# Odd layer's recurrence: sigmoids computed as tanh, and two products whose 128 columns of weights are split into two column halves

## The chip, the cores and the metric

The kernel runs on one core of a Trainium2 chip. Everything is float32. The metric is the device time of one launch in microseconds (us); lower is better.

## The reference, cut to what matters

The program is three transformer blocks in a row on 512 tokens of width 1024. The change lies in the last layer only, the "odd" layer of the third block, in its RWKV-7 recurrence, which runs once forwards and once backwards over the tokens in 16 heads of 64 channels:

```python
def rwkv7_bidir_branch(p, mu, w0, w2, a0, a2, k_k, k_a, r_k, lnx_g, lnx_b):
    q = pf[None] + mu[:, None, None, :] * (shifted - pf[None])
    r, k, v, wd, ad = jnp.split(q, RWKV_SPLITS, axis=-1)
    z_w = w0[:, None, None, :] + jnp.einsum('dbsl,dlc->dbsc', jnp.tanh(wd), w2)
    decay = jnp.exp(-jnp.exp(-jax.nn.softplus(-z_w) - 0.5))      # = exp(-exp(-0.5) * sigmoid(z_w))
    a = jax.nn.sigmoid(a0[:, None, None, :] + jnp.einsum('dbsl,dlc->dbsc', ad, a2))
    kk = heads(k * k_k)
    kk = kk * lax.rsqrt(jnp.maximum(jnp.sum(kk * kk, axis=-1, keepdims=True), 1e-12))
    k = k * (1.0 + (a - 1.0) * k_a)
    ...
def wkv7_step(state, inp):          # scanned over the 512 tokens, with a = -kk, b = kk * a
    r, w, k, v, a, b = inp
    sa = jnp.einsum('...ij,...j->...i', state, a)
    state = (state * w[..., None, :] + sa[..., :, None] * b[..., None, :]
             + v[..., :, None] * k[..., None, :])
    y = jnp.einsum('...ij,...j->...i', state, r)
```

## The kernel before, in words

Each engine has its own instruction list, written out by hand in Python; semaphores between them are numbered by a dry run. The order on an engine is the order in which its generators yield, and no scheduler changes it. ScalarE (ACT) gets a table load wherever the next function isn't in the table set that is loaded.

The recurrence is computed in chunks of 128 tokens, 4 chunks (`NT`) in a sequence. Work is cut into 16 items `i`: item `i` is feature tile `ft = i // 2` (128 channels, so two heads of 64) in direction `d = i % 2`. An item has three stages, and `rw_rounds` runs in one round the chain of item `r`, the inverse of item `r+1` and the products of item `r+2`, interleaved piece by piece, on each of TensorE (PE), ScalarE and VectorE (DVE):

- products (`pe_rw_products`, `act_rw_products`, `dve_rw_products`). PE makes the low-rank products of the decay and of `a` (line 2896). ACT takes their sigmoids into `t_sg` and `t_al` (2961, 2964). DVE scans `t_sg` over a chunk into a running sum `Pc` (3032), takes its tail (3035) and the sum less its middle (3041); ACT makes from them the exponentials s1, s2, s3 (2972, 2973, 2975) and `t_ep`, `t_en` (2978, 2979). Line 2864 and 2869 mix a stream with its shifted self, 2986 squares k, 2846 sums over a head, 2989 takes a root (its own table set), 2857 spreads the result over 64 rows. DVE then forms the four features FM: L3058, L3063 (`b = kk * a`), L3064, L3066, L3069, L3071 (`b` times a decay), L3073, L3078, L3079. PE transposes (2914), multiplies features (2928), and DVE masks the products (`copy_predicated`, 3099). At the end come "rhs own" (line 2946, the masked matrix times the item's own values, 64 columns for each head) and "y own" (2949).
- inverse (`pe_inverse` and its ACT and DVE parts, lines 818 to 939): the triangular inverse of each 128x128 block by doubling, with 64x64 products (833, 849, 861, 869, 878), transposes (818) and copies by ACT (887, 892, 896, 901, 906).
- chain (`pe_rw_chain` and its parts): four steps `n` that depend on each other through the state. A step makes rhs (3168, DVE 3239), u (line 3179: the inverse times rhs, for each of two heads; copied by ACT 3216 in step 0 and by DVE 3244 later), the state update (3187, 3189, DVE 3254 or 3256, 3261) and y (3195, 3197). After every second item DVE, ACT and PE normalise the result (3269 to 3287).

A float32 matmul of the program stands in the trace as two PE records with two weight loads (PEld). So the 8 matmuls of "rhs own" are x16, and the 2 of a u step are x4. "128\*64" in a trace row is the part of the array in use, rows by columns: 128 rows and 64 columns of weights.

POOL zeroes the targets of the masks (3127) and starts inverses (914). After round 13, the last two rounds have no products; other layers' matmuls (line 272) stand beside the chain there.

Of the kernel before, what the change touches and what calls it, by code (L numbers as in the profile page):

```python
# [18 lines left out]
C0 = math.exp(-0.5)  # L19
# [171 lines left out]
def assemble(nc, ctx, io, out):  # L191
# [22 lines left out]
    cols = 53215 - 21 * 128 - NPAR - NROW - 4 * 2048 - 8 * 516 - 64 - 64  # L214
# [10 lines left out]
    def mem_of(ap, width):  # L225
        return View(ap.rearrange("p (a b) -> p a b", b=width))
# [9 lines left out]
    def par(name, k=0):  # L236
        return params[:, PCOL[name] + k:PCOL[name] + k + 1]
# [10 lines left out]
    def bank(*step):  # L248
        return PS[banks.of.get(step, 0)]
# [2559 lines left out]
    om = lambda i: OM[:, i:i + 1]  # L2809
    wv = [mem_of(w, TOK) for w in wbuf]  # L2810
# [74 lines left out]
    def pe_rw_products(pe, i):  # L2885
# [49 lines left out]
        for name, kind in (("rw rhs own", 1), ("rw y own", 2)):  # L2935
            b, before = banks.take(name, i)
            if before:
                pe.wait_ge(*at("out", *before))
            for hd in range(2):
                pe.wait_ge(*at("out", "rw ms", i, 4 * hd + kind))  # L2940
            for c in range(NT):
                s_ = slice(c * 128, (c + 1) * 128)
                for hd in range(2):
                    vs = VK(0)[:, c * 128 + 64 * hd:c * 128 + 64 * hd + 64]
                    if kind == 1:
                        t = pe.mm(PS[b][:, c * 128 + 64 * hd:c * 128 + 64 * hd + 64], MS[hd](1)[:, s_], vs,  # L2946
                                  start=True, stop=True)
                    else:
                        t = pe.mm(PS[b][H2[hd], s_], vs, MS[hd](2)[:, s_], start=True, stop=True)
            t.then_inc(pe.inc(s, "mm", name, i), 1)  # L2950
            yield

    def act_rw_products(a, i):
# [4 lines left out]
        if i:  # L2958
            a.wait_ge(*at("rw kr", i - 1))
        a.wait_ge(*at("mm", "rw w", i))  # L2960
        a.act(t_sg, bank("rw w", i), ACT.Sigmoid, bias=par("o_w0_3", 8 * d + ft)).then_inc(
            a.inc(s, "out", "rw w", i), 1)
        a.wait_ge(*at("mm", "rw a", i))
        a.act(t_al, bank("rw a", i), ACT.Sigmoid, bias=par("o_a0_3", 8 * d + ft)).then_inc(
# [7 lines left out]
        a.act(u3(s1), mdl if d == 0 else u3(s3), ACT.Exp, scale=-C0).then_inc(a.inc(s, "rw s1", i), 1)  # L2972
        a.act(u3(s2), u3(s3) if d == 0 else mdl, ACT.Exp, scale=-C0).then_inc(a.inc(s, "rw s2", i), 1)
        a.wait_ge(*at("rw s2", i))
        a.act(u3(s3), tot, ACT.Exp, scale=-C0).then_inc(a.inc(s, "rw s3", i), 1)
        yield
        a.wait_ge(*at("rw pc", i))
        a.act(t_ep, t_pc, ACT.Exp, scale=-C0).then_inc(a.inc(s, "rw ep", i), 1)
        a.act(t_en, t_pc, ACT.Exp, scale=C0).then_inc(a.inc(s, "rw en", i), 1)
# [39 lines left out]
    def dve_rw_products(v, i):  # L3019
# [11 lines left out]
        for c in range(NT):  # L3031
            v.scan(Pc[:, c, 1:129], ones, t_sg[:, c * 128:(c + 1) * 128], 0.0, MUL, ADD).then_inc(v.inc(s, "rw scan", i), 1)
# [30 lines left out]
        v.tt(FM(3), FM(0), t_al, MUL).then_inc(v.inc(s, "rw b", i), 1)  # L3063
        v.ts(t_al, t_al, par("o_k_a_3", ft), om(50 + ft), MUL, ADD).then_inc(v.inc(s, "rw al", i), 1)  # L3064
# [6 lines left out]
        v.tt(c3(FM(3)), c3(FM(3)), e_k, MUL).then_inc(v.inc(s, "rw f4", i), 1)  # L3071
# [82 lines left out]
    def pe_rw_chain(pe, i):  # L3154
# [5 lines left out]
        for n, c in enumerate(ssd_order(d)):  # L3160
# [17 lines left out]
            for hd in range(2):  # L3178
                t = pe.mm(PS[b][:, 64 * hd:64 * hd + 64], DT(hd)[:, s_], rhs[:, 64 * hd:64 * hd + 64],  # L3179
                          start=True, stop=True)  # L3180
# [159 lines left out]
    def dve_rwkv(v):  # L3340
# [4 lines left out]
        v.ts(OM[:, 50:58], params[:, PCOL["o_k_a_3"]:PCOL["o_k_a_3"] + 8], -1.0, 1.0, MUL, ADD).then_inc(  # L3345
            v.inc(s, "rw mix"), 1)
        v.fill(Pc[:, :, 0:1], 0.0).then_inc(v.inc(s, "rw pc pad"), 1)
# [194 lines left out]
```

## Time and profile before

| | |
|---|---|
| time, median of 3 runs | 4971.45 us (4971.11 to 4972.32) |
| profiled execution, its own time | 4975.08 us |
| its span, first to last instruction | 4973.3 us |
| recurrence, first product to last "rhs own" group | about 3929 to 4690 us of the span |
| PE busy over the span | 4589.2 us (92%) |
| ACT, DVE busy over the span | 845.3 us (17%), 2548.8 us (51%) |
| granted PE clock over the span | 0.928 |

The span of 4973.3 us lies 1.8 us under its execution's own time, and that time lies 3.6 us above the median of the three timed runs. The granted clock is a share of 2.4 GHz: 1.00 is 2.4 GHz, 0.50 is 1.2 GHz, and a value between is a mixture of the two. A row of the chain of waits is start, duration and what ran; a row of the timeline is start, duration, engine, line, operation, operands and count, and behind it the engine's idle time before it with what ended that.

### The profile page before, as it was taken

Reading aid. Unit: us, or ns where it says so; the run is one execution under the profiler, and the core shown is the slowest. Engines: PE = TensorE matmul, PEld = TensorE weight load, DVE = VectorE, ACT = ScalarE, POOL = GpSimd, SP = SyncE. Lnnn points to the kernel's source line nnn. Section 1 sums busy time; section 2 is a strip of 40 time slices with the busy share of each in tenths; the row PEclk is TensorE's granted clock in tenths of the full one; section 3 lists DMA queues with packets and bytes.
Section 4 is the critical chain, followed back from the end, with each engine's and each line's share of the span. In section 5 each row is a group of like instructions: output and inputs, shape, how many; then the busy total and the mean of one; then the engine's idle time right before and its main releaser. Section 6 shows DMA issues by size and latency. Waiting matters only on the chain.

```text
span 4973.3 us, 64889 instructions
## 1 busy us (share of the span) xinstructions
PE 4589.2 (92%) x28316; PEld 3408.7 (69%) x28316; DVE 2548.8 (51%) x4403; ACT 845.3 (17%) x1490; POOL 123.6 (2%) x228
## 2 busy tenths in 40 slices
PE   9999998879998999799989999989999788888899
PEld 7886445557886888356656488858887666666644
DVE  5675865334545456553344265556454355555511
ACT  0001023111022000321222100011000233333210
POOL 0000000000000000000000000000000011111000
PEclk9998999868999999899999999989899888878899
DMA  6524442004222222111111222222222000000021
GB/s 238 179 94 58 65 65 51 1 1 85 93 86 67 85 91 87 36 41 51 51 43 35 68 85 85 68 85 86 67 88 77 27 2 2 2 2 2 19 96 42
DMA packets 284954, 311.69 MB, mean 63 GB/s; under 512 B 7168, under 2 KB 277632, under 8 KB 281600
## 3 DMA queue, kind: packets, MB, share of 16 engines
q1 hardware_dynamic: 284672, 307.55, 21.7%
q8 instruction: 223, 3.65, 0.3%
q14 instruction: 59, 0.48, 0.0%
HBM read 305.43 MB, written 2.10 MB: 62 GB/s over the span
## 4 chain that ended last, share of the span: by engine, by line
PE 49%; DVE 5%; ACT 3%; issue 1%; DMA 0%; POOL 0%; DVEq 0%; POOLq 0%; ACTq 0%; SPq 0%
PE ps L348 18%; PE ps L272 13%; PE ps L2125 1%; PE ps L317 1%; PE ps L833 1%; PE ps L471 1%; PE ps L2928 1%; PE ps L2857 1%; PE ps L849 1%; PE ps L3179 1%; PE ps L2846 1%; PE ps L2946 1%; PE ps L818 1%; PE ps L1845 1%; PE ps L2665 1%
## 5 line engine op out<-in xcount | busy, mean ns | idle before, releaser
L272 PE MATMUL ps<-main,w 128*128 128x512 f32 (+1 forms) x2832 | 1245.2, 596 | 21.9 <-DMA w<-in_ffn_wg 12.2
L348 PE MATMUL ps<-main 128*128 128x256 f32 x5136 | 1139.2, 379 | 0.0
L348 PEld LDWEIGHTS ps<-main 128*128 128x128 f32 x5136 | 975.5, 190 | 133.1
L272 PEld LDWEIGHTS ps<-main,w 128*128 128x128 f32 x2832 | 543.2, 195 | 647.3 <-issue 619.6
L348 PE MATMUL ps<-main,w 128*128 128x256 f32 x3872 | 863.9, 379 | 1.4 <-DVE main L416 1.4
L348 PEld LDWEIGHTS ps<-main,w 128*128 128x128 f32 x3872 | 736.1, 190 | 105.8 <-issue 4.3
L435 DVE TENSOR_TENSOR main<-main,ps 128x512 f32<-128x512 f32 x164 | 112.8, 688 | 417.7 <-PE ps L348 417.5
L661 DVE SCALAR_TENSOR_TENSOR main<-main,params_sb 128x512 f32<-128x512 f32 x256 | 192.5, 752 | 9.1
L387 ACT COPY main<-ps 128x256 f32<-128x256 f32 x98 | 36.5, 372 | 896.3 <-PE ps L348 896.3
L432 DVE TENSOR_TENSOR main<-main,ps 128x512 f32<-128x512 f32 x98 | 67.3, 687 | 221.6 <-PE ps L348 218.8
L440 DVE TENSOR_TENSOR main<-main,ps 128x512 f32<-128x512 f32 x164 | 112.8, 688 | 78.0 <-PE ps L348 76.7
L397 DVE TENSOR_TENSOR main<-w 128x512 f32<-128x512 f32 (+1 forms) x164 | 111.2, 678 | 31.2 <-DMA w<-in_w_in 11.8
L849 PE MATMUL ps<-main 64*64 64x64 f32 x3200 | 86.7, 261 | 32.2 <-ACT main L892 26.4
L402 DVE TENSOR_TENSOR main<-w,main 128x512 f32<-128x512 f32 (+1 forms) x164 | 112.4, 686 | 5.6
L400 DVE TENSOR_TENSOR main<-main,w 128x512 f32<-128x512 f32 (+1 forms) x164 | 112.4, 685 | 5.7
L398 DVE TENSOR_TENSOR main<-w 128x512 f32<-128x512 f32 (+1 forms) x164 | 111.1, 677 | 0.0
L849 PEld LDWEIGHTS ps<-main 64*64 64x64 f32 x3200 | 71.9, 167 | 54.7 <-issue 24.3
L387 ACT COPY tmp<-ps 128x256 f32<-128x256 f32 x66 | 24.6, 372 | 498.9 <-PE ps L348 498.9
L533 ACT ACTIVATE tmp<-main 128x512 f32<-128x512 f32 x104 | 63.8, 629 | 266.1 <-DVE main L585 79.0
L2179 DVE TENSOR_TENSOR main<-main 128x512 f32<-128x512 f32 x56 | 38.8, 692 | 135.3 <-PE ps L2125 126.9
L3099 DVE COPY_PREDICATED w<-consts_sb,ps 128x512 f32<-128x512 uint32 x128 | 85.6, 724 | 43.3 <-PE ps L2928 43.3
L818 PE MATMUL ps<-consts_sb,main 128*128 128x128 f32 x400 | 83.1, 343 | 23.0 <-DVE main L919 23.0
(456 smaller groups left out, 4985.2 us busy)
## 6 DMA issues: line engine op xcount, KB each, us to landing
w<-in_w_in SPq DMA_DIRECT2D x58, 1024.0 KB, 7.0
w<-in_e_w_in SPq DMA_DIRECT2D x28, 1024.0 KB, 5.0
main<-in_ada_w SPq DMA_DIRECT2D x24, 1024.0 KB, 5.0
w<-in_ffn_wg SPq DMA_DIRECT2D x22, 1024.0 KB, 6.4
w<-in_ffn_wu SPq DMA_DIRECT2D x22, 1024.0 KB, 6.3
w<-in_o_w_in SPq DMA_DIRECT2D x20, 1024.0 KB, 5.5
w<-in_ffn_wd SPq DMA_DIRECT2D x16, 1024.0 KB, 5.1
w<-in_w_up SPq DMA_DIRECT2D x16, 1024.0 KB, 5.5
```

The costliest lines, as they stand in the source:

```text
L272: i = pe.mm(PS[b][:, 0:n], wv[:, k, f * 128:(f + 1) * 128], g.X(kg + k), start=kg + k == 0, stop=kg + k == g.nk - 1)
L348: t = pe.mm(PS[b][:, 256 * half:256 * half + 256], weight[:, m, :], x(m), start=m == 0, stop=m == n - 1)
L397: v.tt(S[0], a21, a22, ADD).then_inc(v.inc(s, "sum 0", *step), 1)
L398: v.tt(S[2], a21, a11, SUB).then_inc(v.inc(s, "sum 2", *step), 1)
L400: v.tt(S[1], S[2], a22, ADD).then_inc(v.inc(s, "sum 1", *step), 1)
L402: v.tt(S[3], a12, S[1], SUB).then_inc(v.inc(s, "sums", *step), 1)
L435: v.tt(inner, two(c[3]), b[2], ADD).then_inc(v.inc(s, "most", *step), 1)
L440: v.tt(inner, inner, b[3], ADD).then_inc(v.inc(s, "out", "seven", 3, *step), 1)
L661: v.stt(out, src[:, j:j + TOK], w(j), out, MUL, ADD).then_inc(v.inc(s, "tap", j, *step), 1)
L818: t = pe.tp(part128(PS[b], n), part128(src, n), ident)
L849: t = pe.mm(PS[two[e][0]][HALF[q], 64 * n:64 * n + 64], E4[HALF[e], n, q, :], X4[HALF[e], n, q, :], start=True, stop=True)
L3099: v.pick(c3(MS[hd](kind)), mid(const(strict if kind < 2 else incl), 4).bitcast(U32), c3(bank("rw ms", i, k))).then_inc(v.inc(s, "out", "rw ...
```

## The change

Sigmoid(x) is (1 + tanh(x/2)) / 2. ACT now computes tanh of half the argument, with halved biases that DVE prepares once in a small tile `HW` (two more DVE instructions at the start). The factor 1/2 and the added 1 are taken up by what follows: the scan adds `ones` at each step instead of multiplying by it (`ADD, ADD`), so the running sum is twice the old one, and the five exponentials have half the scale; `b` is `(tanh + 1) * kk`, halved where it is multiplied by its decay; the constants of the line that makes `1 + (a - 1) k_a` are halved. Two `tensor_tensor` become `scalar_tensor_tensor`.

In "rhs own" (kind 1) and in the u step, each matmul with 128 columns of weights becomes two with 64 columns of weights each, for the upper and the lower half of the output's partitions, one straight after the other. All 128 rows and all 64 moving columns stay.

`cols` now counts the constants by `NCON`, so that `main` has room for `HW`; nothing else moves in memory.

```diff
@@ -2943,8 +2945,9 @@  (pe_rw_products)
                     if kind == 1:
-                        t = pe.mm(PS[b][:, c * 128 + 64 * hd:c * 128 + 64 * hd + 64], MS[hd](1)[:, s_], vs,
-                                  start=True, stop=True)
+                        for h in HALF:
+                            t = pe.mm(PS[b][h, c * 128 + 64 * hd:c * 128 + 64 * hd + 64],
+                                      part128(MS[hd](1), c)[:, h], vs, start=True, stop=True)
@@ -2957,11 +2960,12 @@  (act_rw_products)
+        a.wait_ge(*at("rw half"))
         a.wait_ge(*at("mm", "rw w", i))
-        a.act(t_sg, bank("rw w", i), ACT.Sigmoid, bias=par("o_w0_3", 8 * d + ft)).then_inc(
+        a.act(t_sg, bank("rw w", i), ACT.Tanh, scale=0.5, bias=hw(8 * d + ft)).then_inc(
...
-        a.act(t_al, bank("rw a", i), ACT.Sigmoid, bias=par("o_a0_3", 8 * d + ft)).then_inc(
+        a.act(t_al, bank("rw a", i), ACT.Tanh, scale=0.5, bias=hw(16 + 8 * d + ft)).then_inc(
...
-        a.act(u3(s1), mdl if d == 0 else u3(s3), ACT.Exp, scale=-C0).then_inc(a.inc(s, "rw s1", i), 1)
+        a.act(u3(s1), mdl if d == 0 else u3(s3), ACT.Exp, scale=-C0 / 2).then_inc(a.inc(s, "rw s1", i), 1)
...
@@ -3029,7 +3033,7 @@  (dve_rw_products)
-            v.scan(Pc[:, c, 1:129], ones, t_sg[:, c * 128:(c + 1) * 128], 0.0, MUL, ADD).then_inc(v.inc(s, "rw scan", i), 1)
+            v.scan(Pc[:, c, 1:129], ones, t_sg[:, c * 128:(c + 1) * 128], 0.0, ADD, ADD).then_inc(v.inc(s, "rw scan", i), 1)
...
-        v.tt(FM(3), FM(0), t_al, MUL).then_inc(v.inc(s, "rw b", i), 1)
-        v.ts(t_al, t_al, par("o_k_a_3", ft), om(50 + ft), MUL, ADD).then_inc(v.inc(s, "rw al", i), 1)
+        v.stt(FM(3), t_al, 1.0, FM(0), ADD, MUL).then_inc(v.inc(s, "rw b", i), 1)
+        v.ts(t_al, t_al, hw(32 + ft), om(50 + ft), MUL, ADD).then_inc(v.inc(s, "rw al", i), 1)
...
-        v.tt(c3(FM(3)), c3(FM(3)), e_k, MUL).then_inc(v.inc(s, "rw f4", i), 1)
+        v.stt(c3(FM(3)), c3(FM(3)), 0.5, e_k, MUL, MUL).then_inc(v.inc(s, "rw f4", i), 1)
@@ -3176,8 +3180,9 @@  (pe_rw_chain)
             for hd in range(2):
-                t = pe.mm(PS[b][:, 64 * hd:64 * hd + 64], DT(hd)[:, s_], rhs[:, 64 * hd:64 * hd + 64],
-                          start=True, stop=True)
+                for h in HALF:
+                    t = pe.mm(PS[b][h, 64 * hd:64 * hd + 64], part128(DT(hd), c)[:, h], rhs[:, 64 * hd:64 * hd + 64],
+                              start=True, stop=True)
@@ -3342,8 +3347,12 @@  (dve_rwkv)
+        v.ts(HW[:, 0:32], params[:, PCOL["o_w0_3"]:PCOL["o_w0_3"] + 32], 0.5, None, MUL).then_inc(
+            v.inc(s, "rw half w"), 1)
+        v.ts(HW[:, 32:40], params[:, PCOL["o_k_a_3"]:PCOL["o_k_a_3"] + 8], 0.5, None, MUL).then_inc(
+            v.inc(s, "rw half"), 1)
```

Two places show what it does to the instruction lists. The first is ACT at the start of item 3's products, from the first function after the low-rank products to the copy for the inverse. Before:

```order
L2961 ACT_TABLE_LOAD [waits pe_rwkv]
L2961 ACTIVATE tmp<-ps,params_sb 128x512 [waits dve_rwkv]
L2964 ACTIVATE tmp<-ps,params_sb 128x512 [waits pe_rwkv]
L3216 ACTIVATE main<-ps 128x128 [waits pe_rwkv]
L2972 ACT_TABLE_LOAD
L2972 ACTIVATE small<-small 128x4 [waits dve_rwkv]
L2973 ACTIVATE small<-main 128x4
L2975 ACTIVATE small<-main 128x4 [waits act_rwkv]
L887 COPY main<-ps 128x512 [waits pe_rwkv]
```

The same place in the changed kernel (line 2965 is the old 2961, 2968 the old 2964, 3221 the old 3216, 2976 to 2979 the old 2972 to 2975):

```order
L2965 ACT_TABLE_LOAD [waits pe_rwkv]
L2965 ACTIVATE tmp<-ps,main 128x512 [waits dve_rwkv]
L2968 ACTIVATE tmp<-ps,main 128x512 [waits pe_rwkv]
L3221 ACTIVATE main<-ps 128x128 [waits pe_rwkv]
L2976 ACTIVATE small<-small 128x4 [waits dve_rwkv]
L2977 ACTIVATE small<-main 128x4
L2979 ACTIVATE small<-main 128x4 [waits act_rwkv]
L887 COPY main<-ps 128x512 [waits pe_rwkv]
```

The load ahead of the exponentials is gone, the one ahead of the tanh stays where the one ahead of the sigmoid was. Over the whole program the table loads go from 94 to 77: one in each of the 16 items, and in the first item both, since a tanh stands ahead of it already.

The second place is PE in the round that follows, from the end of one item's products into the chain's first u step and, further on, its second. Before:

```order
L2946 MATMUL ps<-main,w 128x64 x7
L2949 MATMUL ps<-w,main 64x128 x8
L2896 MATMUL ps<-main 128x512 x2
L3179 MATMUL ps<-main 128x64 [waits act_rwkv,dve_rwkv]
L3179 MATMUL ps<-main 128x64
...
L2846 MATMUL ps<-consts_sb,tmp 128x2 x3
L3179 MATMUL ps<-main 128x64 [waits dve_rwkv]
L3179 MATMUL ps<-main 128x64
L833 MATMUL ps<-main,w 64x64 [waits dve_rwkv]
```

In the changed kernel (2949, 2952, 2898, 3184 and 2848 are the old 2946, 2949, 2896, 3179 and 2846):

```order
L2949 MATMUL ps<-main,w 64x64 x15
L2952 MATMUL ps<-w,main 64x128 x8
L2898 MATMUL ps<-main 128x512 x2
L3184 MATMUL ps<-main 64x64 [waits act_rwkv,dve_rwkv]
L3184 MATMUL ps<-main 64x64 x3
...
L2848 MATMUL ps<-consts_sb,tmp 128x2 x3
L3184 MATMUL ps<-main 64x64 [waits dve_rwkv]
L3184 MATMUL ps<-main 64x64 x3
L833 MATMUL ps<-main,w 64x64 [waits dve_rwkv]
```

In these rows 128x64 is the output, partitions by columns, and a matmul counts once. The places, the waits and the neighbours are the same; 8 matmuls became 16 and 2 became 4.

## Rows read from the trace of the kernel before

**Rows 1.** Busy by stretch: start:end, length, busy of PE, PEld, DVE, ACT, POOL, PEclk.
```profile
3929.50:4690.00 760.50, 626.38 (x9235) 504.24 (x9236) 432.77 (x1072) 275.77 (x476) 108.89 (x183) 0.82 0.01 2
4230.00:4246.00 16.00, 14.57 (x292) 12.49 (x291) 10.22 (x24) 4.48 (x8) 2.70 (x3) 1.00 0.01 2
4252.00:4275.00 23.00, 18.51 (x253) 15.17 (x254) 14.88 (x41) 10.19 (x19) 1.42 (x3) 0.61 0.01 2
```

**Rows 2.** Chain of waits over 3929.5 to 4690 us, its shares by line.
```profile
by line: PE ps L2928 5.5%; PE ps L2857 5.2%; PE ps L833 5.2%; PE ps L471 5.2%; PE ps L849 4.7%; PE ps L3179 4.5%; PE ps L2846 4.4%; PE ps L2946 4.2%; PE ps L818 3.5%; PE ps L2896 3.0%; DVE tmp L2869 2.8%; ACT L2972 2.7%; DVE main L914 2.4%;
```

**Rows 3.** The same chain in order of time, parts of one round.
```profile
4253.66 1.28 ACT L2972
...
4261.10 0.95 PE ps L3179 x4
...
4272.64 1.09 PE ps L3179 x4
...
4274.79 2.00 PE ps L471 x2
...
4294.60 1.93 PE ps L2946 x16
4296.53 0.84 PE ps L2846 x8
```

**Rows 4.** Timeline of ACT, DVE and PE around the load of line 2972.
```profile
4252.93 1.37 DVE L3032 TENSOR_TENSOR_SCAN main<-consts_sb,tmp 128x128 f32<-128x128 f32 x4 [6.42 <-ACT tmp L2961]
4253.66 1.28 ACT L2972 ACT_TABLE_LOAD   x1
4254.33 0.17 DVE L3035 TENSOR_TENSOR small<-main 128x4 f32<-128x4 f32 x1
4254.61 0.70 DVE L3041 TENSOR_TENSOR tmp<-main,small 128x516 f32<-128x516 f32 x1
4254.95 0.21 ACT L2972 ACTIVATE small<-small 128x4 f32<-128x4 f32 x1
4255.87 0.64 ACT L2978 ACTIVATE tmp<-tmp 128x516 f32<-128x516 f32 x1
4256.02 1.13 PE L833 MATMUL ps<-main,w 64*64 64x64 f32 x32 [0.91 <-ACT main L887]
```

**Rows 5.** Timeline of PE, 128\*64 work of another stage with 64 moving columns.
```profile
2408.05 3.89 PE L2125 MATMUL ps<-main 128*64 128x64 f32 x64 [3.77 <-ACT main L2102]
...
2477.20 1.15 PE L2150 MATMUL ps<-main 128*64 128x64 f32 x16
...
2486.21 2.16 PE L2125 MATMUL ps<-main 128*64 128x64 f32 x64
```

**Rows 6.** Timeline of PE where 128\*128 work is followed by 128\*64 work.
```profile
4738.69 0.39 PE L3189 MATMUL ps<-main 128*128 128x128 f32 x2
4738.91 0.39 PE L3195 MATMUL ps<-main 128*128 128x128 f32 x2
4739.23 0.44 PE L3197 MATMUL ps<-w,main 128*64 128x128 f32 x4
```

**Rows 7.** Timeline of PE and DVE around u steps and what follows them.
```profile
4226.86 0.74 DVE L3079 SCALAR_TENSOR_TENSOR tmp<-tmp,params_sb 128x512 f32<-128x512 f32 x1
4227.81 2.07 PE L471 MATMUL ps<-tmp,consts_sb 128*128 128x512 f32 x2
...
4260.96 1.09 PE L3179 MATMUL ps<-main 128*128 128x64 f32 x4
4261.98 1.13 PE L833 MATMUL ps<-main,w 64*64 64x64 f32 x32
...
4273.47 0.74 DVE L3079 SCALAR_TENSOR_TENSOR tmp<-tmp,params_sb 128x512 f32<-128x512 f32 x1
```

**Rows 8.** Groups of instructions on DVE, the two forms that are exchanged.
```profile
L3063 DVE TENSOR_TENSOR w<-main,tmp 128x512 f32<-128x512 f32 x16 | 11.1, 692 | 0.5
...
L758 DVE SCALAR_TENSOR_TENSOR main<-main 128x512 f32<-128x512 f32 x16 | 10.3, 688 | 0.3
```

More of the change, by code:

```diff
@@ L213, in assemble @@
     small = sb("small", [128, 64])
-    cols = 53215 - 21 * 128 - NPAR - NROW - 4 * 2048 - 8 * 516 - 64 - 64
+    cols = 53215 - NCON - NPAR - NROW - 4 * 2048 - 8 * 516 - 64 - 64
     main = sb("main", [128, cols])[:, :]
@@ L2809, in assemble @@
     om = lambda i: OM[:, i:i + 1]
+    HW = mem(37184, 1, 64).ap[:, 0, :]
+    hw = lambda i: HW[:, i:i + 1]
     wv = [mem_of(w, TOK) for w in wbuf]
@@ L2971, in act_rw_products @@
         a.wait_ge(*at("rw tail", i))
-        a.act(u3(s1), mdl if d == 0 else u3(s3), ACT.Exp, scale=-C0).then_inc(a.inc(s, "rw s1", i), 1)
-        a.act(u3(s2), u3(s3) if d == 0 else mdl, ACT.Exp, scale=-C0).then_inc(a.inc(s, "rw s2", i), 1)
+        a.act(u3(s1), mdl if d == 0 else u3(s3), ACT.Exp, scale=-C0 / 2).then_inc(a.inc(s, "rw s1", i), 1)
+        a.act(u3(s2), u3(s3) if d == 0 else mdl, ACT.Exp, scale=-C0 / 2).then_inc(a.inc(s, "rw s2", i), 1)
         a.wait_ge(*at("rw s2", i))
-        a.act(u3(s3), tot, ACT.Exp, scale=-C0).then_inc(a.inc(s, "rw s3", i), 1)
+        a.act(u3(s3), tot, ACT.Exp, scale=-C0 / 2).then_inc(a.inc(s, "rw s3", i), 1)
         yield
         a.wait_ge(*at("rw pc", i))
-        a.act(t_ep, t_pc, ACT.Exp, scale=-C0).then_inc(a.inc(s, "rw ep", i), 1)
-        a.act(t_en, t_pc, ACT.Exp, scale=C0).then_inc(a.inc(s, "rw en", i), 1)
+        a.act(t_ep, t_pc, ACT.Exp, scale=-C0 / 2).then_inc(a.inc(s, "rw ep", i), 1)
+        a.act(t_en, t_pc, ACT.Exp, scale=C0 / 2).then_inc(a.inc(s, "rw en", i), 1)
         yield
@@ L3344, in dve_rwkv @@
         v.ts(OM[:, 0:50], mu, -1.0, 1.0, MUL, ADD).then_inc(v.inc(s, "rw mix mu"), 1)
-        v.ts(OM[:, 50:58], params[:, PCOL["o_k_a_3"]:PCOL["o_k_a_3"] + 8], -1.0, 1.0, MUL, ADD).then_inc(
+        v.ts(OM[:, 50:58], params[:, PCOL["o_k_a_3"]:PCOL["o_k_a_3"] + 8], -0.5, 1.0, MUL, ADD).then_inc(
             v.inc(s, "rw mix"), 1)
+        v.ts(HW[:, 0:32], params[:, PCOL["o_w0_3"]:PCOL["o_w0_3"] + 32], 0.5, None, MUL).then_inc(
+            v.inc(s, "rw half w"), 1)
+        v.ts(HW[:, 32:40], params[:, PCOL["o_k_a_3"]:PCOL["o_k_a_3"] + 8], 0.5, None, MUL).then_inc(
+            v.inc(s, "rw half"), 1)
         v.fill(Pc[:, :, 0:1], 0.0).then_inc(v.inc(s, "rw pc pad"), 1)
```

## The prediction, made before the changed kernel ran

> **What bounds the kernel now.** I read the busy times by stretch first, then the chain of waits, then the timeline where the chain passes the changed lines. The whole program is bound by PE (92% of the span), but the change lies in one stretch of 760 us, and there PE is busy for 626 us only, at a granted clock of 0.82 [rows 1]. So time is lost in two ways there: PE waits for ACT and DVE, and after such waits it runs for a while at 1.2 instead of 2.4 GHz (a clock of 0.61 between 4252 and 4275 us, where ACT and DVE hand work to and fro, against 1.00 between 4230 and 4246 us, where PE is busy for 14.6 of 16 us [rows 1]). The chain of waits in this stretch is a mixture of short pieces of all three engines, of which the changed lines hold: u (L3179) 4.5%, "rhs own" (L2946) 4.2%, the table load (L2972) 2.7% [rows 2]. In order of time the reader is to see that each round (760 us for 16 items) passes through one load, one L2946 and three u steps, of which the load, two u steps and L2946 are shown [rows 3].
>
> **Part 1, the table load.** There are 16 loads of 1.28 us ahead of the exponentials, all on the chain (2.7% of 760 us is 20.5 us) [rows 2, 3]. Not all of it is won. The exponential behind the load needs DVE's tail, L3035, which ends at 4254.50, while the load ends at 4254.94 [rows 4]: the scan (4 instructions, 1.37 us) runs beside the load. Without it the exponential starts at about 4254.53, 0.42 us earlier than 4254.95. The next possible stop is L2978, which needs L3041 (ends 4255.31) and would then stand at 4255.87 - 0.42 = 4255.45, so it isn't held [rows 4]. Two things are released by this ACT stretch: PE's L833 through the copy L887, for which it waits 0.91 us [rows 4], and the mixing of k, so the 0.42 us is on the path. The other 14 rounds show the same distances within 0.02 us; only in item 0 DVE's L3041 ends with the load, and nothing is won. Sum: 15 x 0.42 = 6.3 us. Bounds: 0 (if PE's own queue were the limit, which its wait speaks against) and 16 x 1.28 = 20.5 us. The load ahead of the tanh stays, and its waits too. The load that goes in item 0 stood beside the low-rank products and hid there.
>
> The Trainium skill (ScalarE: Activation LUTs, "What ACT_TABLE_LOAD costs") counts a switch at about 2.66 us, of which 1.38 us is a drain. The trace doesn't agree: the activation behind the load starts 1.29 us after the load [rows 4]. By that rule the sum would not change either where DVE's tail is the next to be waited for.
>
> **Part 2, the form of the products.** No row shows these two lines in the new form, but L2125 is that form exactly: 128 rows, 64 columns of weights, 64 moving columns, the two column halves in turn. It takes 2.16 us for 64 records, 0.034 us each, at full clock, and 3.89 us, 0.061 us each, after a wait at the low one [rows 5]. L2946 takes 1.93 us for 16 records, 0.12 us each, and L3179 0.95 to 1.09 us for 4 at the low clock [rows 3]. The count of records doubles.
>
> A change between forms of the array costs something. L3189 and L3195 are both 128\*128 and start 0.22 us apart; L3195 and the 128\*64 L3197 start 0.32 us apart, for as many records [rows 6]. So 0.10 us for a change at full clock.
>
> "Rhs own": 32 x 0.034 = 1.08 us instead of 1.93, 0.85 us less. In items of direction 0 the next work (L2949) is 128\*64 too, and a change goes away rather than comes. In the others L2846 (128\*128) stands behind it [rows 3], one change more, 0.75 us less. All 16 are on the chain (4.2% of 760 us is 31.9 us, 2.0 us each [rows 2]). Nothing that follows is late: the masks and transposes that L2949 and L2846 need are done before L2946 starts. Sum: 8 x 0.85 + 8 x 0.75 = 12.8 us.
>
> u, step by step. Step 0 is followed by a wait for ACT (L3216 behind the two sigmoids), step 3 by DVE's masks and by L3244 queued behind them: nothing is won. Step 1 runs after L2846 and ahead of L833; start to start it takes 1.02 us [rows 7]. New: 8 x 0.061 = 0.49 us, and two changes instead of one, at the low clock perhaps 0.15 us each, an estimate from the 0.10: about 0.8 us, 0.2 us less. At full clock (3 rounds of 14) 8 x 0.034 us plus 0.2 leaves 0.1 us. Step 2 is the same, but L471 behind it needs DVE's L3079: in most rounds that ends at 4274.21 against a start of L471 at 4274.79 on the chain [rows 3, 7], so there is room for 0.2 us; in the three rounds like the one at 4227 us it ends at 4227.60 against 4227.81, and less a hand-over of 0.14 us only 0.07 us is left [rows 7]. Sum: step 1 gives 11 x 0.2 + 3 x 0.1 = 2.5 us, step 2 gives 11 x 0.2 + 3 x 0.07 = 2.4 us, together 4.9 us. Bounds: 22 x 0.53 = 11.7 us if changes of form cost nothing (1.02 - 0.49), and 0 if they cost all. In the last two rounds u stands between the full-array products of line 272; eight narrow records and two changes cost what four wide ones do. Nothing.
>
> **Part 3, DVE.** Two tensor_tensor become scalar_tensor_tensor with a constant: 692 against 688 ns [rows 8], so 0. A scan that adds instead of multiplies, other constants and a bias from another tile: 0. Two small instructions at the start stand beside the load of the low-rank weights, for which PE waits: 0. If each of the two exchanged forms cost the 0.05 us more that forms with a per-channel scalar show (0.74 us [rows 7]), it would be 1.6 us.
>
> **Sum.** 6.3 + 12.8 + 4.9 = 24.0 us. The profiled execution took 4975.1 us in all, span 4973.3; it would be 4951.1. It lies 3.6 us above the median of the timed runs, 4971.45, so I predict 4947 us.
>
> **Rivals.**
> Halves don't overlap. L2150 has the same form, but all the records of a group go to one half: 1.15 us for 16, 0.072 us each [rows 5]. If the new lines ran at that pace, "rhs own" would take 2.3 us, 0.37 us more, 16 times 5.9 us; u about 0.2 us more, 28 times 5 us; with part 1 taken off, about 5 us slower: 4976 us. Against it stands L2125, whose order of halves is the one that is written here. The Trainium skill (TensorE: Matmul & The Clock Gate, "Part 3: Packing small matmuls") says that weight loads overlap running matmuls only when the row group differs, and both halves have the same rows; by that rule this rival would hold. L2125's 0.034 us beside L2150's 0.072 us says that it doesn't. Chance 6%.
>
> Changes of form cost more than I count. Then u gives nothing and "rhs own" some 9 us: 6.3 + 9 = 15 us, 4956 us. For it: pieces of one form between others are everywhere in a round, and 0.10 us comes from one place. Chance 22%. The Trainium skill (TensorEngine Tiling, "Key Properties") says that changing the tiling mode drains the TensorE; rows 6 agree in sign with 0.10 us.
>
> They cost less, and u gives its bound: 6.3 + 13 + 11 = 30 us, 4941 us. Chance 16%.
>
> The slower side: the clock. PE gets less to do before each wait. If a quarter of the 14.6 us that PE works at full clock between 4230 and 4246 us [rows 1] fell to 1.2 GHz in every round, that would add 15 x 3.6 = 55 us: 31 us slower, 5002 us. It decides from 24/15 = 1.6 us of such work a round, and is slower by more than 0.2% from 2.3 us on. For it: the clock does fall in every round, to 0.61 in the stretch that follows [rows 1], and nothing in the trace says how near to falling it is before that. Against it: the wait gets shorter by part 1, and the work is as dense as before. Chance 5%. A smaller drift of the clock that gives back 14 to 24 us: 6%, about 4966 us.
>
> The table load would not go: the instruction list shows that it does.
>
> **Numbers.** The forecast has 45%, with a range of its own of 4940 to 4954. Faster by over 0.2% (10 us, about what can be told from no change) are it and the two variants: 83%. Within 0.2%: halves that don't overlap and the smaller drift, 12%. Slower: 5%. The range of 8 in 10 runs from 4936 to 4962.
>
> **What would show it.** L2946's line x512 in 128\*64 form, about 1.1 us a group, busy some 18 us instead of 33; L3179's x512, at the low clock about 0.7 to 0.8 us start to start; no load on line 2976, and the exponential 0.03 us behind DVE's tail; rounds of about 47 us; PEclk of the stretch within 0.02 of 0.82. I am wrong if the narrow records take 0.07 us each, if the clock of the stretch falls below 0.79, or if the chain goes through other engines at the place of L2946.

## The result, and the profile after

The changed kernel takes 4927.01 us (median of 4 runs, 4925.46 to 4934.56), the kernel before beside it 4971.89 us (4971.11 to 4972.49): a ratio of 0.9913, 95% interval 0.9896 to 0.993, or 44.9 us less. The forecast was 4947 us with a range of 4936 to 4962. The direction was right, the size nearly double, and the time lies below the range.

| | before | after |
|---|---|---|
| profiled execution, its own time | 4975.08 us | 4927.05 us |
| span | 4973.3 us | 4925.3 us |
| from the first low-rank product to the end | 1043.8 us | 999.7 us |
| of it at 1.2 GHz ("low"), summed from the trace's clock record | 286.7 us in 37 pieces | 238.9 us in 33 pieces |
| mean round of the recurrence (14 rounds) | 48.1 us | 45.3 us |

A piece of low time that reaches into this stretch is counted whole; the last piece, in which the program ends, is left out.

44.1 of the 48.0 us between the two profiled executions lie in the recurrence and what follows; 3.9 us lie ahead of it, in code that is the same.

The changed lines answer to [rows 3, 5, 8] as groups by form (busy us and mean ns behind the bar, then idle time before them):

```profile
L3184 PE MATMUL ps<-main 128*64 128x64 f32 x512 | 34.8, 269 | 4.2 <-DVE main L3244 4.0
L2949 PE MATMUL ps<-main,w 128*64 128x64 f32 x512 | 18.4, 224 | 1.5 <-DVE w L3103 1.5
L3067 DVE SCALAR_TENSOR_TENSOR w<-tmp,main 128x512 f32<-128x512 f32 x16 | 11.1, 692 | 0.5
L3075 DVE SCALAR_TENSOR_TENSOR w<-w,tmp 128x512 f32<-128x512 f32 x16 | 10.9, 684 | 0.0
L471 PE MATMUL ps<-tmp,consts_sb 128*128 128x512 f32 x44 | 34.9, 885 | 24.8 <-DVE tmp L491 16.8 <-DVE tmp L3083 7.9
```

The same groups before:

```profile
L3179 PE MATMUL ps<-main 128*128 128x64 f32 x256 | 53.2, 344 | 8.7 <-DVE main L3239 8.6
L2946 PE MATMUL ps<-main,w 128*128 128x64 f32 x256 | 32.9, 283 | 1.5 <-DVE w L3099 1.5
L471 PE MATMUL ps<-tmp,consts_sb 128*128 128x512 f32 x44 | 41.4, 1041 | 24.0 <-DVE tmp L491 16.8 <-DVE tmp L3079 7.1
```

"Rhs own" (L2949) is busy for 18.4 us, where L2946 had 32.9; u (L3184) for 34.8 us, where L3179 had 53.2. The exchanged DVE forms cost what the old ones did. But L471, which nobody changed, went from 41.4 to 34.9 us.

The start of a round answers to [rows 4]:

```profile
4228.95 1.37 DVE L3036 TENSOR_TENSOR_SCAN main<-consts_sb,tmp 128x128 f32<-128x128 f32 x4 [5.14 <-ACT tmp L2965]
4230.35 0.17 DVE L3039 TENSOR_TENSOR small<-main 128x4 f32<-128x4 f32 x1
4230.55 0.20 ACT L2976 ACTIVATE small<-small 128x4 f32<-128x4 f32 x1 [0.89 <-DVE small L3039]
4231.47 0.64 ACT L2982 ACTIVATE tmp<-tmp 128x516 f32<-128x516 f32 x1
```

The load is gone, ACT now waits 0.89 us for DVE's tail L3039, and the exponential starts 0.03 us behind it. From the scan to L2982 it is 2.52 us, before it was 2.94: 0.42 us, as forecast.

The u step and "rhs own", answering to [rows 3, 7]; the second fence is from the chain of waits:

```profile
4236.63 0.70 PE L3184 MATMUL ps<-main 128*64 128x64 f32 x8
4237.26 1.13 PE L833 MATMUL ps<-main,w 64*64 64x64 f32 x32
...
4258.98 0.45 PE L3184 MATMUL ps<-main 128*64 128x64 f32 x8
4259.36 0.69 PE L833 MATMUL ps<-main,w 64*64 64x64 f32 x32
```

```profile
4269.63 1.08 PE ps L2949 x32
4270.71 0.98 PE ps L2848 x8
```

u takes 0.63 us start to start at the low clock (1.02 before, 0.8 forecast) and 0.38 at the full one; "rhs own" 1.08 us, where the chain before had 1.93 [rows 3].

Where else did time go? Item 4's round in both kernels, cut in pieces of 15 us (the columns are those of [rows 1]; the number behind POOL's is the granted clock). Before, then after:

```profile
4154.89:4169.89 15.00, 11.75 (x151) 9.80 (x155) 7.28 (x23) 8.79 (x16) 1.49 (x4) 0.66 0.00 1
4169.89:4184.89 15.00, 11.03 (x164) 8.38 (x164) 11.04 (x28) 2.77 (x5) 0.00 (x0) 0.77 0.00 1
4184.89:4199.89 15.00, 14.84 (x262) 12.53 (x263) 9.21 (x19) 3.55 (x6) 3.23 (x4) 1.00 0.01 3
4199.89:4207.19 7.30, 5.86 (x45) 3.80 (x44) 2.46 (x5) 2.57 (x5) 3.85 (x8) 0.68 0.01 2
```

```profile
4139.74:4154.74 15.00, 11.60 (x154) 9.41 (x154) 7.83 (x24) 7.51 (x15) 1.50 (x4) 0.66 0.01 1
4154.74:4169.74 15.00, 12.30 (x252) 9.85 (x254) 11.37 (x31) 3.36 (x6) 0.00 (x0) 0.89 0.01 2
4169.74:4184.74 15.00, 13.30 (x246) 11.08 (x240) 9.07 (x20) 5.17 (x9) 5.16 (x9) 1.00 0.01 2
```

The clock falls in the same place at the start of the round. Later it is back earlier (0.89 against 0.77), and the fall that ended the old round (0.68) doesn't come. Lines that are the same in both kernels show what that is worth. Before, then after:

```profile
4177.27 2.07 PE L471 MATMUL ps<-tmp,consts_sb 128*128 128x512 f32 x2
...
4203.17 1.97 PE L2857 MATMUL ps<-consts_sb,main 128*64 128x128 f32 x16 [1.44 <-DVE main L3280]
4205.07 2.08 PE L2896 MATMUL ps<-main 64*128 64x512 f32 x4
```

```profile
4161.15 1.13 PE L471 MATMUL ps<-tmp,consts_sb 128*128 128x512 f32 x2
...
4184.18 1.09 PE L2859 MATMUL ps<-consts_sb,main 128*64 128x128 f32 x16 [1.43 <-DVE main L3285]
4185.20 1.13 PE L2898 MATMUL ps<-main 64*128 64x512 f32 x4
```

Each of the three is 0.9 us shorter because TensorE runs at 2.4 instead of 1.2 GHz. No term of the forecast held such a gain.

### The profile page after: what moved, and what is told of

Read it like the earlier page. It is cut to its first block, busy times and chain, and to the rows that moved or that the text cites. A ratio compares the mean times of both kernels' runs of the same rounds, so it can differ in the third digit from the quotient of the medians.

```text
span 4925.3 us, 65898 instructions
## 1 busy us (share of the span) xinstructions
PE 4542.3 (92%) x28828; PEld 3368.0 (68%) x28828; DVE 2548.0 (52%) x4405; ACT 823.5 (17%) x1473; POOL 123.7 (3%) x228
## 4 chain that ended last, share of the span: by engine, by line
PE 48%; DVE 5%; ACT 3%; issue 1%; DMA 0%; POOL 0%; DVEq 0%; POOLq 0%; ACTq 0%; SPq 0%
PE ps L348 19%; PE ps L272 13%; PE ps L2125 1%; PE ps L317 1%; PE ps L833 1%; PE ps L2930 1%; PE ps L2859 1%; PE ps L2848 1%; PE ps L471 1%; PE ps L849 1%; PE ps L818 1%; PE ps L1845 1%; PE ps L2665 1%; PE ps L1834 1%; DVE main L3036 0%
## 5 line engine op out<-in xcount | busy, mean ns | idle before, releaser
L348 PEld LDWEIGHTS ps<-main,w 128*128 128x128 f32 x3872 | 736.1, 190 | 105.8 <-issue 4.3
L397 DVE TENSOR_TENSOR main<-w 128x512 f32<-128x512 f32 (+1 forms) x164 | 111.2, 678 | 31.2 <-DMA w<-in_w_in 12.3
```

Of the source, the lines that this page charges most:

```text
L348: t = pe.mm(PS[b][:, 256 * half:256 * half + 256], weight[:, m, :], x(m), start=m == 0, stop=m == n - 1)
L397: v.tt(S[0], a21, a22, ADD).then_inc(v.inc(s, "sum 0", *step), 1)
```

## The experiments

Theory: the change is worth in place about what was forecast (24 us), and the rest of the 45 us is time at 1.2 GHz that no longer occurs. Rival: all of it is work saved in place, and a term was mis-sized. "In place" means: at the changed lines themselves, with the clock the same in both kernels. "Low" is the time at 1.2 GHz of the profiled execution, counted as in the table above; before has 286.7 us of it.

| kernel | us, median (lowest to highest) | ratio to before, 95% | low, us |
|---|---|---|---|
| tanh only | 4971.23 (4968.22 to 4974.45) | 0.9998 [0.9989, 1.0007] | 303.8 |
| rhs own in halves only | 4958.42 (4956.39 to 4959.32) | 0.9974 [0.9963, 0.9984] | 276.5 |
| u in halves only | 4959.50 (4955.84 to 4961.09) | 0.9974 [0.9965, 0.9984] | 266.2 |
| both halves | 4939.87 (4938.36 to 4942.24) | 0.9937 [0.9922, 0.9952] | 249.2 |
| all three (the change) | 4927.01 (4925.46 to 4934.56) | 0.9913 [0.9896, 0.993] | 238.9 |
| halves in a row | 4936.59 (4929.94 to 4937.59) | 0.9929 [0.9913, 0.9946] | 228.7 |
| head sums in halves | 4902.52 (4901.61 to 4903.38) | 0.9864 [0.9849, 0.9879] | 208.2 |
| one matmul more | 4932.75 (4931.48 to 4934.33) | 0.9925 [0.991, 0.994] | 221.9 |
| two matmuls more | 4958.25 (4954.01 to 4960.55) | 0.9975 [0.9964, 0.9985] | 276.5 |
| before, filled | 4926.25 (4924.88 to 4927.78) | 0.9912 [0.9897, 0.9927] | 95.6 |
| tanh only, filled | 4919.83 (4913.78 to 4919.92) | 0.9896 [0.9881, 0.991] | 105.8 |
| after, filled | 4893.82 (4886.38 to 4895.16) | 0.9843 [0.9829, 0.9858] | 75.1 |
| filled at the products' waits | 4924.56 (4919.28 to 4924.78) | 0.99 [0.9886, 0.9915] | 204.8 |
| filled at the chain's waits | 4900.23 (4893.78 to 4910.26) | 0.9856 [0.984, 0.9872] | 88.7 |
| before, filled, head sums in halves | 4909.36 (4908.05 to 4911.81) | 0.9871 [0.9855, 0.9888] | 88.7 |
| after, filled, head sums in halves | 4869.02 (4862.97 to 4870.38) | 0.9794 [0.9779, 0.9809] | 47.8 |

### The parts of the change, each alone

The two products put back to their old form in the changed kernel (tanh only); here the edit in "rhs own", the one in u is its like:

```diff
-                        for h in HALF:
-                            t = pe.mm(PS[b][h, ...], part128(MS[hd](1), c)[:, h], vs, start=True, stop=True)
+                        t = pe.mm(PS[b][:, ...], MS[hd](1)[:, s_], vs, start=True, stop=True)
```

> The changed kernel with the wide form of both products put back: only the tanh part is left. Theory A (each edit saves in its own place what the trace of the changed kernel shows there, and what is left of the 45 us comes from TensorE's clock, which falls and rises at other places once the rounds have another length): 0.41 us a round in place, 6 us, so 4966 us, give or take some 10 us of clock that need not have the sign of the edit; the load on the line of the exponentials gone, the exponential 0.41 us earlier, and whatever differs beyond that sits in PE pieces that run at 1.2 in one kernel and 2.4 GHz in the other. Theory B (the parts simply are worth more than I priced, and add up to 45 us): 10 to 15 us faster, spread evenly over the rounds, and the time at the low clock as before.

Its first 700 us of the recurrence:

```profile
3924.60:4624.60 700.00, 579.03 (x8450) 465.04 (x8450) 399.55 (x991) 234.16 (x423) 100.70 (x171) 0.81 0.01 2
```

From the first function of a round to the exponential it takes 2.32 us instead of 2.74, in all rounds but the first two (2.58 before), and yet the kernel isn't faster: the clock is 0.81, with 17 us more at 1.2 GHz. This was the first sign that the clock matters as much as the work.

The other way round, one product at a time in the kernel before, and both:

```diff
-                        t = pe.mm(PS[b][:, ...], MS[hd](1)[:, s_], vs, start=True, stop=True)
+                        for h in HALF:
+                            t = pe.mm(PS[b][h, ...], part128(MS[hd](1), c)[:, h], vs, start=True, stop=True)
```

> The kernel before with the column halves in rhs own alone. Theory A: 16 groups of 1.1 instead of 2.0 us, 13 us in place, 4959 us, plus or minus the clock's share. Theory B: 18 to 22 us faster. Either way the line's busy time falls from 32.9 to about 18 us.

> The kernel before with the column halves in the u step alone. Theory A: 0.17 us in step 1 and up to 0.28 us in step 2 of each of 14 rounds, 4 to 6 us, 4966 us, plus or minus the clock's share. Theory B: the line is busy 18 us less in the changed kernel, so 15 to 18 us faster, 4955 us.

> The kernel before with the column halves in both products, and the sigmoids kept. Theory A: 13 + 6 = 19 us in place, 4953 us, and the sum of the differences of e1, e2 and e3 misses the 45 us of the whole change by several us, since the clock's share doesn't add up. Theory B: about 4972 - 45 + (what e1 gives), and e2 and e3 add up to it within 3 us.

Measured: 13.5, 12.5 and 32.1 us less than before. For u alone and for both, neither theory had the number (4 to 6 or 15 to 18 us expected for u). The three parts alone add up to 0.7 + 13.5 + 12.5 = 26.7 us; the whole gives 44.9. So the parts aren't additive, and what is missing in the sum is missing in the low time too. Alone, the parts change it by +17.1, -10.2 and -20.5 us, 13.6 us less together; the whole takes 47.8 us off. At 0.4 us for each microsecond at the low clock, a price that is worked out below, these 34.2 us are 14 of the 18.2 us that are missing.

### TensorE's waits filled

The waits of TensorE were filled with useless matmuls. They (256 columns, a constant times the identity, into an unused half of the bank, where nobody reads it) stand ahead of five waits in each item. The comments in this cut are added here.

```diff
+    def pe_fill(pe, b, n, o=256):
+        for _ in range(n):
+            pe.mm(PS[b][:, o:o + 256], ident, consts[:, 0:256], start=True, stop=True)
...
+        if name[0] == "rw kk":            # head sums of k
+            pe_fill(pe, b, 1)
...
+        if name[0] == "rw rstd all":      # spread behind the root
+            pe_fill(pe, b, 3)
...
+                if n == 2:                # third rhs of the chain
+                    pe_fill(pe, b, 3)
...
+                if n == 0:                # first state update
+                    pe_fill(pe, b, 3)
...
+            if m == 2 and name[0] == "rw":    # the inverse's second level
+                pe_fill(pe, two[0][0], 2)
```

> The kernel before with full-array matmuls of no use put into the places where PE waits in a round (3 ahead of the first state update, 2 ahead of the inverse's first product, 1 ahead of the head sums of k, 3 ahead of the third rhs, 3 ahead of the spread in the normalising; each writes columns of a bank that nobody reads). Theory A (the clock's share): PE's granted clock in the recurrence rises from 0.82 to 0.90 or more, the first L471 of a round takes 1.1 instead of 2.0 us, and the kernel gets 20 to 50 us faster although it does more. Theory C (what was gained beyond the priced terms has nothing to do with the clock): the clock may rise, the time doesn't fall below 4968 us.

> The changed kernel with the same matmuls in the same places. Theory A: with the clock held up in both, the difference between this and the filled kernel before is what the edits save in place, about 20 to 25 us (0.41 us of ACT, 0.85 us of rhs own and about 0.3 us of u a round), and no longer 45 us. Theory C: the difference stays 40 us or more.

> The kernel before with the tanh instead of the sigmoids and with the useless matmuls at TensorE's waits, products in their old form. Its partner is the kernel before with these matmuls, 4926.25 us. Theory (the tanh saves 0.41 us in place in 15 items, and without the filling the clock took this back): 6 us less than the partner, 4916 to 4923 us. Rival (the saving of 0.41 us is not on the path, it only lengthens a wait elsewhere): 4926 us, no difference to the partner within 2 us.

The same 700 us, of before filled and of after filled:

```profile
3927.00:4627.00 700.00, 616.72 (x9448) 490.75 (x9450) 426.58 (x1065) 273.01 (x471) 108.69 (x183) 0.94 0.01 2
```

```profile
3927.40:4627.40 700.00, 614.54 (x10444) 483.63 (x10444) 444.04 (x1113) 257.02 (x465) 108.74 (x183) 0.95 0.01 4
```

The kernel before gets 45.2 us faster by work that nobody needs, while the clock rises from 0.82 to 0.94. That the clock is worth tens of microseconds here is shown by this. The tanh, worth 0.7 us without the filling, is worth 6.4 us with it (4926.25 less 4919.83). That this is the forecast's 6.3 is partly luck: the low time differs by 10.2 us, the other way. At 0.4 us for each, the profiled executions of the two tanh pairs, from the first low-rank product to the end, give 7.0 us in place with the filling (2.9 + 4.1) and 7.4 without (0.6 + 6.8). The whole change is worth 32.4 us, above the 20 to 25 expected: the low time still differs by 20.5 us. All five places cost something too: the low time falls by 191 us, at 0.4 some 76, and the time only by 45.

### A pair nearly without time at the low clock

Filling and the head sums of line 2846 in column halves, on both kernels:

```diff
-            t = pe.mm(PS[b][:, 2 * c:2 * c + 2], x[:, c * 128:(c + 1) * 128], head_sums, start=True, stop=True)
+            for h in HALF:
+                t = pe.mm(PS[b][h, 2 * c:2 * c + 2], part128(x, c)[:, h], head_sums, start=True, stop=True)
```

> The changed kernel with the useless matmuls at TensorE's waits and with the head sums in two column halves. It tells whether the 24.5 us that the head sums in halves gave were in place or the clock's. In place they measured 26.7 less 16.0, that is 10.7 us, at a mixed clock; with the clock held up (0.95) the same records are shorter, so 6 to 11 us: 4883 to 4888 us. Rival (all 24.5 us are in place, behind the sums): 4869 us. It is also the fastest version that the runs so far point to.

> The kernel before with the useless matmuls at TensorE's waits and the head sums in two column halves: the partner of the changed kernel with both, 4869.02 us, whose recurrence spends 41 us at the low clock. Between these two the clock should have little part, so the difference is what the change is worth in place. Theory (the change gives 24 to 27 us in place: tanh 6, rhs own 12.6, u 5 to 9; the rest of the measured 45 us was the clock): 4893 to 4897 us, if the time at the low clock comes to 40 to 60 us here too. Rival (all of the 45 us are in place): 4914 us.

In medians the pair stands 40.3 us apart, not 24 to 27: the kernel before with both took 4909.36 us, not 4893 to 4897, nearer to what the rival said (4914). But its low time isn't the 40 to 60 us that the theory asked for, it is 88.7, and the two still differ by 40.9 us. The rounds tell work and clock apart. Of the kernel before with both:

```profile
4183.73:4225.86 42.13, 38.35 (x636) 31.11 (x637) 26.39 (x68) 17.52 (x31) 6.23 (x11) 1.00 0.01 2
4225.86:4271.60 45.74, 40.97 (x655) 32.09 (x653) 29.12 (x74) 17.66 (x31) 7.89 (x15) 0.96 0.01 2
4362.90:4404.74 41.84, 38.06 (x635) 30.85 (x636) 26.38 (x68) 17.52 (x30) 5.94 (x11) 1.00 0.01 2
4404.74:4451.59 46.85, 42.73 (x656) 33.18 (x654) 29.21 (x74) 17.67 (x31) 8.19 (x16) 0.93 0.01 2
4493.79:4538.01 44.22, 39.73 (x656) 31.03 (x654) 29.03 (x74) 17.67 (x32) 8.19 (x16) 1.00 0.01 2
```

Of the changed kernel with both:

```profile
4449.54:4492.03 42.49, 37.95 (x685) 29.34 (x685) 29.02 (x74) 16.38 (x30) 8.19 (x16) 1.00 0.01 3
4492.03:4532.31 40.28, 36.31 (x671) 29.04 (x672) 26.33 (x68) 16.23 (x30) 5.95 (x11) 1.00 0.01 2
```

Rounds at full clock from end to end are 41.84 and 44.22 us (the two directions) before, 40.28 and 42.49 after: 1.56 and 1.73 us less, 1.65 on average, 24.7 us for 15 rounds. The forecast's sum was 24.0. The 24.7 us are good to about 2 us: the row of 42.13 us is at 1.00 too, and with such rounds in the mean the sum is up to 1.2 us larger; and with the head sums in halves "rhs own" saves 0.95 us in both directions, in the change itself 0.75 us in one of them (below), about 1.4 us less in all. The same rows price the clock. Of three rounds of one direction the one at 1.00 takes 44.22 us, the one at 0.96 takes 45.74, the one at 0.93 takes 46.85. By the clock 0.04 of 45.74 us is 2 × 0.04 × 45.74 = 3.7 us at 1.2 GHz for 1.52 us of time, and 2 × 0.07 × 46.85 = 6.6 us for 2.63 us: 0.4 us for each microsecond at the low clock. With it the pair adds up: from the first low-rank product to the end the profiled executions are 40.5 us apart (983.2 and 942.7), and 24.7 + 0.4 × 40.9 = 41.1.

The Trainium skill (TensorE: Matmul & The Clock Gate, "HAM oscillation — how this bites in real kernels") counts half of the throttled time as lost. The rounds agree in kind and give 0.4. TensorE is busy for 40.97 of the 45.74 us of such a round, so part of the low time can fall on its waits; that this makes the difference isn't shown.

The expectation of the changed one was wrong: 4883 to 4888 us without a part of the clock, 4869.02 measured, the number of the rival. Its low time says where the rest comes from: 27 us less than with the filling alone (75.1 to 47.8). It is the fastest version found, 0.9794 of before [0.9779, 0.9809] and 58 us under the changed kernel.

### Head sums in halves, halves in a row

> The changed kernel with the same column halves in the head sums too (128 columns of weights and 2 moving columns, now 64 and 64). At the low clock, where the group of k stands, 16 records of 0.061 us and a change of form instead of 8 of 0.23 us: 1.1 instead of 1.87 us, and nothing for the warm group of the variance; 0.7 us for 15 rounds, 10 us in place, 4917 us, and with Theory A plus or minus several us of clock. If the fixed time of a record decides at 2 moving columns, 16 records take as long as 8 did and more: 4930 us.

```profile
L2849 PE MATMUL ps<-consts_sb,tmp 128*64 128x2 f32 x256 | 16.0, 246 | 15.3 <-ACT tmp L2991 15.3
```

The expectation was 10 us. The sums of k take 16.0 us instead of 28.2 in the changed kernel, 11 to 12 us less, at a time that fell by 24.5. The low time fell by 30.7 us, at 0.4 another 12.

> The changed kernel, with the 16 matmuls of rhs own ordered so that the 8 of one column half come first and then the 8 of the other. If the alternation is what lets the loads of 64 columns overlap (0.034 against 0.072 us a record in the kernel before): a group takes 2.2 to 2.3 us instead of 1.1, 17 to 19 us in all, 4945 us. If loading 64 instead of 128 columns is all that counts: no change, 4927 us.

```diff
-            for c in range(NT):
...
-                for hd in range(2):
+            for h, c, hd in ([(h, c, hd) for h in HALF for c in range(NT) for hd in range(2)] if kind == 1 else
+                             [(None, c, hd) for c in range(NT) for hd in range(2)]):
...
-                        for h in HALF:
```

```profile
L2949 PE MATMUL ps<-main,w 128*64 128x64 f32 x512 | 30.4, 224 | 1.5 <-DVE w L3103 1.5
```

All of one column half first: 30.4 us against 18.4, 0.059 us a record against 0.036. Less than the 0.072 of L2150 [rows 5], and the time rose by 9.6 us, not 17 to 19: 12.0 us in place, less what the clock gave back (low time 10 us less, 4 us), is 8. The old wide form was busy for 32.9 us, so nearly all of the gain is the order and not the narrower weights. The start times of the records show how: in turn, two records start 0.007 us apart and the next two 0.05 to 0.06 us later; in a row, mostly one starts every 0.058 us. So the rival of the forecast ("halves don't overlap") is real as a mechanism, but only where one half follows itself; the order that is written keeps clear of it. The Trainium skill (TensorE: Matmul & The Clock Gate, "Part 3: Packing small matmuls") has weight loads overlap only where the row group differs; here both forms have the same rows, and the order of the column halves alone makes 0.059 or 0.036.

### A small dose of work

One or two matmuls of 128 columns, of no use, between the wait of the head sums of k and the head sums, in each item of the changed kernel. They stand behind the wait, so they fill none:

```diff
+        if name[0] == "rw kk":
+            for _ in range(2):
+                pe.mm(PS[b][:, 256:384], ident, x[:, 0:128], start=True, stop=True)
```

> The changed kernel with one useless full-array matmul of 128 columns (two records) more ahead of each item's head sums of k, 16 in all. In place it costs 0.1 us at full clock or 0.25 us at the low one, 16 times 1.6 to 4 us. Theory (what a small edit is worth depends on where the pieces at 1.2 GHz come to lie): the time moves by another amount than these 2 to 4 us, up or down by some 5 to 20 us, and the time spent at the low clock (239 us of the recurrence in the changed kernel) moves with it. Rival (the clock's share follows the work alone): 4929 to 4931 us and the same share.

> The same with two of these matmuls in each item. In place 3 to 8 us. Rival (in proportion): 4930 to 4935 us, twice the step of the kernel with one. Theory (the places of the low clock shift): no such proportion between the two kernels; one of them may even be faster than the changed kernel, since the added work stands ahead of a wait.

```profile
4248.71 1.22 PE L2849 MATMUL ps<-tmp,consts_sb 128*128 128x128 f32 x4 [0.29 <-ACT tmp L2993]
4249.72 1.71 PE L2851 MATMUL ps<-consts_sb,tmp 128*128 128x2 f32 x8
```

The dose is larger than I had thought: two matmuls take 1.01 us there at the low clock, and the head sums start 0.57 and 1.01 us later in the mean round, 8.6 and 15.2 us for 15. The time rose by 5.7 and by 31.2 us. The first dose costs less than its work, the second one 25.5 us for 6.6 us more. The low time moves with it: 17 us less than in the changed kernel with one, 37.6 us more with two, and 15.2 + 0.4 × 37.6 = 30 us. For one it adds up less well: 8.6 - 0.4 × 17 = 2 us against 5.7.

### Which waits

> The changed kernel with useless matmuls at two of the five places only: one ahead of the head sums of k and three ahead of the spread behind the root, both waits of the products for ScalarE. Theory (the clock is given back wherever TensorE stands and waits, and the low stretch behind these two waits is the longest of a round): most of the gain of all five places, which was 33 us: 4896 to 4908 us. Rival (the gain is shared evenly): 14 us, 4913 us.

> The other three places only: ahead of the first state update, of the inverse's second level and of the third rhs. Theory: 5 to 15 us of the 33, 4912 to 4922 us. Rival (even shares): 20 us, 4907 us. If this kernel and its partner add up to more or less than 33 us, the clock's share isn't additive between places either.

```profile
3927.00:4627.00 700.00, 581.62 (x9639) 461.30 (x9640) 427.43 (x1063) 250.26 (x452) 108.68 (x183) 0.86 0.01 2
```

```profile
3926.00:4626.00 700.00, 596.93 (x10262) 474.56 (x10266) 442.67 (x1108) 256.61 (x464) 108.70 (x183) 0.94 0.01 4
```

I had it the wrong way round. The products' waits, where the clock stands low, gave 2.5 us of the 33.2; the chain's and the inverse's gave 26.8 (4896 to 4908 and 4912 to 4922 us expected, 4924.56 and 4900.23 measured). The first of these kernels is at 0.86, the second at 0.94. Filling where the clock is seen low doesn't say that it fell for that wait. Which of the three places does it wasn't tried. The second kernel's four runs took 4894.20, 4910.26, 4893.78 and 4906.27 us, at clocks of 0.948, 0.944, 0.948 and 0.945: one program, two levels 12 us or more apart. So its gain is 33 us at one level and 17 to 21 us at the other, and on both far more than 2.5. The profile is of the faster level. The two fillings also differ in amount, 4 matmuls an item against 8; equal amounts weren't tried.

## Why the prediction was wrong in size

**Table load, 6.3 us: right.** 0.42 us a round against [rows 4]. One reading was off: item 1 doesn't show the same distances. Its load starts 0.56 us behind the scan, not 0.73, and wins 0.25 us, so the sum is 14 × 0.42 + 0.25 = 6.1 us. The two tanh pairs gave 7.0 and 7.4 us in place.

**"Rhs own", 12.8 us: right.** Where the head sums follow, it takes from start to start 1.08 us instead of 1.83, 0.75 us less as forecast. Where "y own" follows, here in the pair with filling and head sums in halves, before and after:

```profile
4574.39 2.00 PE L2957 MATMUL ps<-main,w 128*128 128x64 f32 x16
4576.32 1.09 PE L2960 MATMUL ps<-w,main 128*64 128x128 f32 x16
```

```profile
4527.85 1.15 PE L2960 MATMUL ps<-main,w 128*64 128x64 f32 x32
4528.83 1.05 PE L2963 MATMUL ps<-w,main 128*64 128x128 f32 x16
```

Start to start 1.93 us and 0.98 us, 0.95 us less (0.85 forecast); before and after show the same in all items but the first. 7 × 0.75 + 8 × 0.95 = 12.9 us.

**u, 4.9 us: right within its bounds.** Step 1 saves more than forecast (0.4 us at the low clock, forecast 0.2), because the eight narrow records and their changes of form take 0.63 us together, not 0.8. Step 2, in the rounds at full clock, saves nothing: from DVE's first feature to L471 it is 8.08 us in both filled kernels, L471 waits for DVE. Of the 1.56 and 1.73 us of a full-clock round 0.42 are the tanh's and 0.95 "rhs own"'s, which leaves some 0.2 to 0.4 for u.

**The sum, 24.0 us: right in place (24.7 us, give or take 2), wrong as a forecast of the time.** The step that failed is the clock, a term that the sum put at nothing. The forecast held it fixed ("PEclk of the stretch within 0.02 of 0.82") and let it move only as a loss, in two rivals with 11% together. Over the first 700 us it moved by 0.02, from 0.82 to 0.84, and that was enough: to the end 47.8 us less at 1.2 GHz, at 0.4 us each 19 us, and 24.7 + 19 = 44, measured 44.1. A tolerance of 0.02 over the 760 us of [rows 1] is 2 × 0.02 × 760 = 30 us at the low clock, 12 us of time: as much as the whole range of the forecast allowed on that side (11 us). So the forecast's own sign of being right let in a miss of this size. The trace of before held the hint: a mean of 0.82, made of 37 separate low pieces, each of which could come to lie elsewhere.

A fit of twelve of the kernels (recurrence to the end as a sum of tanh, rhs own, u, head sums, filling and low time) gives 0.47 ± 0.03 us for each microsecond at the low clock, 8.8 ± 0.5, 9.9 ± 0.8 and 3.3 ± 1.0 us for the three parts, 22.0 together, with a scatter of 0.8 us. It takes the parts to be additive, and puts more on the tanh and less on "rhs own" than their own lines show; the total is the firmer number. So the part in place lies between 22 and 26 us, the clock's between 18 and 22.

**Rivals.** Halves that don't overlap: false in this order, true in a row. Changes of form that cost more: false. Costs of form at nothing (4941 us): near for step 1 of u, and still 14 us above the time. The clock: the right mechanism with the wrong sign.

Still open: why the low pieces shift as they do. The tanh alone adds 17 us of them, both halves take 37 us off, and the tanh on top of the halves takes off another 10. No rule in the traces gave the sign beforehand; the doses of work show that it changes between 0.57 and 1.01 us of added work a round. Why a low microsecond costs 0.4 in single rounds and 0.47 in the fit is open too.

## What to carry to other kernels

Where TensorE works at a mixed clock as it does here, a forecast from saved work needs a second term, which here was as large as the first, with a sign that the saved work didn't tell (+17 us of low time for the tanh, -10 and -20 for the products). Price it from the trace (here 0.4 us for each us at 1.2 GHz), widen the range by it on both sides, and judge an edit by a pair of kernels that both hold the clock up, since unfilled the tanh looked worthless. And try to hold it up: useless matmuls at a few waits gave as much as this change did. Products with few moving columns (64 and 2 here) gained by being split in alternating column halves.

## What the hardware showed that I had not expected

- TensorE with more to do made the same program 45.2 us faster (clock 0.82 to 0.94).
- The place of the filling matters: 4 useless matmuls an item at the products' waits give 2.5 us, 8 at the chain's and the inverse's 26.8 us, 0.6 against 3.4 us for each of the four or eight.
- The eight records of the head sums have 2 moving columns each and yet take 1.64 us from start to start at the low clock (from 4249.72 above), 0.2 us each, hardly less than the 0.24 to 0.27 of L3179's records with 64 columns [rows 3]. So their time doesn't go by the columns. In column halves all 16 take 0.49 us at full clock in the changed kernel with filling, where the eight took 0.98 us.
- Records of 64 columns of weights take 0.036 us with the column halves in turn and 0.059 us in a row. In turn they start in twos, 0.007 us apart.
- Adding 6.6 us of work to the kernel with one useless matmul an item cost 25.5 us.
